# Behind the expert loop: fewer returned rows summed on TensorE, turned tiles copied out by ScalarE

## The reference

```
x = x + gt2 * moe_ffn(modulate(rmsnorm(x, g_ffn[l]), ...), ...)   # 6 of 64 experts a token, and a shared one
...
return rmsnorm(x, g_final)                                        # end of first_block
...
xn = rmsnorm_2(h, norm_mix_g)                                     # start of second_block
proj = jnp.einsum('bsd,de->bse', xn, w_in) + b_in
```

## Time and profile before

| | |
|---|---|
| three runs | 2151.91, 2157.5 and 2158.29 us; median 2157.5 us |
| the profiled execution | 2153.83 us, span 2152.1 us |
| mean granted TensorE clock | 0.992 of full speed |
| busy share of the span | TensorE 95%, VectorE 46%, ScalarE 18%, GpSimd 10% |
| the stretch behind the expert loop | from about 1203 us to the barrier's end at 1259.6 us |

### The profile page before, as it was taken

One profiled execution on the slowest core, in us unless ns is written; L12 is line 12 of the kernel. 1 busy time (PEld: TensorE's weight loads), 2 busy tenths in 40 slices (PEclk: granted clock), 3 DMA queues, 4 the chain that ended last, 5 costly groups with the idle time before them and its releaser, 6 DMA issues. The chain is left out here.

```text
span 2152.1 us, 34202 instructions
## 1 busy us (share of the span) xinstructions
PE 2053.5 (95%) x13624; PEld 1343.3 (62%) x13624; DVE 981.1 (46%) x2048; ACT 384.0 (18%) x832; POOL 213.8 (10%) x281
## 2 busy tenths in 40 slices
PE   6999999999889999999999989999999999999998
PEld 2455567885456666666666444555888668885443
DVE  2554346654532222222222388543655354546564
ACT  3113434441211111111111120111111110000000
POOL 7000023420001111111111000000000000000000
PEclk9999999999999999999999999999999999999999
DMA  9631010020459999999999632103222222223442
GB/s 393 255 118 39 1 41 3 3 74 17 163 223 401 422 421 413 408 403 399 390 387 362 273 151 83 60 30 118 79 79 79 78 79 79 109 87 137 176 172 102
DMA packets 56444, 392.99 MB, mean 183 GB/s; under 512 B 11864, under 2 KB 11992, under 8 KB 21008
## 3 DMA queue, kind: packets, MB, share of 16 engines
q1 hardware_dynamic: 43376, 366.02, 43.1%
q0 software_dynamic: 12960, 25.42, 3.1%
HBM read 385.93 MB, written 27.26 MB: 192 GB/s over the span
## 5 line engine op out<-in xcount | busy, mean ns | idle before, releaser
L2251 PE MATMUL bank<-arena 128*128 128x512 f32 x448 | 198.2, 600 | 2.4 <-SPq L2224 2.4
L2347 PE MATMUL bank<-arena 128*128 128x256 f32 x896 | 194.1, 379 | 0.5 <-DVE arena L2838 0.5
L2418 PE MATMUL bank<-arena 128*128 128x256 f32 x896 | 193.6, 379 | 0.1
L2458 PE MATMUL bank<-arena 128*128 128x512 f32 x448 | 192.7, 592 | 0.1
L2347 PEld LDWEIGHTS bank<-arena 128*128 128x128 f32 x896 | 170.1, 190 | 24.8 <-DVE arena L2838 0.9
L2418 PEld LDWEIGHTS bank<-arena 128*128 128x128 f32 x896 | 170.2, 190 | 23.3 <-issue 0.3
L1662 PE MATMUL bank<-arena 128*64 128x256 f32 x704 | 159.8, 381 | 19.8 <-DMA arena<-in_wexp 14.6
L1649 PE MATMUL bank<-arena 128*128 128x128 f32 x1408 | 163.0, 276 | 2.5 <-ACT arena L1755 0.3
L1649 PEld LDWEIGHTS bank<-arena 128*128 128x128 f32 x1408 | 158.9, 191 | 7.6 <-issue 6.9
L1664 PE MATMUL bank<-arena 128*64 128x256 f32 x704 | 160.3, 382 | 0.0
L2458 PEld LDWEIGHTS bank<-arena 128*128 128x128 f32 x448 | 85.1, 190 | 107.2 <-issue 106.2
(11 more groups left out here) (582 smaller groups left out, 2849.1 us busy)
## 6 DMA issues: line engine op xcount, KB each, us to landing
arena<-in_wexp SPq DMA_DIRECT2D x198, 1024.0 KB, 19.6
arena<-in_w2f SPq DMA_DIRECT2D x24, 2048.0 KB, 7.4
arena<-in_wmod SPq DMA_DIRECT2D x12, 2048.0 KB, 9.0
arena<-in_w2j SPq DMA_DIRECT2D x8, 2048.0 KB, 7.4
arena<-in_win SPq DMA_DIRECT2D x6, 2048.0 KB, 10.9
arena<-expert_rows SPq DMA_DIRECT2D x12, 1024.0 KB, 15.7
arena<-in_w2t SPq DMA_DIRECT2D x8, 1536.0 KB, 6.5
arena<-in_x SPq DMA_DIRECT2D x2, 2048.0 KB, 10.1
```

Source lines behind the costliest of these rows:

```text
L2251: mm = pe.matmul(bk, wv[:, k, :], rhs[:, k, :], start=(k == 0), stop=(k == nk - 1))
L2347: mm = pe.matmul(bk[:, 0:HT], lhs[:, k, :], right[:, k, :], start=(first and k == 0), stop=(k == nk - 1), skip_group_check=not last or not ...
L2418: mm = pe.matmul(b[:, 0:HT], lhs(k), rhs(k), start=(first and k == 0), stop=(k == 3), skip_group_check=not last or not first)
L2458: mm = pe.matmul(b[:, :], lhs(f), rhs(f), start=(g % 8 == 0 and f == 0), stop=(g % 8 == 7 and f == 1))
```

## The change

Two things are moved. First, TensorE sums rows 0, 1 and 2 of a tile, and VectorE adds row 3 itself, ahead of its other adds. Second, the copying out of the turned tiles goes to ScalarE: since its scale is one value per partition, and each block of 128 columns has its own column of `g2`, a tile takes eight instructions of 128 x 128 in place of two of 128 x 512. They stand, for the tile before, ahead of the scaled copy of the row (`xr`). Of the last tile ScalarE copies the second bank, and VectorE the first.

```diff
                 for c in range(2):
                     pe.wait_ge(S(f"yd_in{t}{c}"), 16)
                     for half in range(2):
-                        for k in (2 * c, 2 * c + 1):
-                            mm = pe.matmul(bank[2 * t + half][:, :], ident, y[:, k, 512 * half:512 * half + 512], start=False, stop=(k % 2 == 1),
+                        for k in ((0, 1), (2,))[c]:
+                            mm = pe.matmul(bank[2 * t + half][:, :], ident, y[:, k, 512 * half:512 * half + 512], start=False, stop=(k >= 1),
                                            skip_group_check=True)
...
+            def turned_out(t, ks):
+                for k in ks:
+                    act.wait_ge(S("xn1_mm"), 2 * t + k // 4 + 1)
+                    act.activation(tail_xnT[:, k, t * P:(t + 1) * P], bank[2 * t + k // 4][:, (k % 4) * P:(k % 4 + 1) * P], ACT.Copy, scale=col2("g2", k))
+
...
                 act.wait_ge(S("tail_rs"), t + 1)
+                if t >= 1:
+                    turned_out(t - 1, range(KD))
                 act.activation(xr[:, t, :], xs[:, t, :], ACT.Copy, scale=tail_rs[:, t, 0:1]).then_inc(S("tail_xr"), 1)
+            turned_out(NT_X - 1, range(4, KD))
...
                 y = yslot[t].rearrange("p (k d) -> p k d", k=TOP_K)
+                dve.wait_ge(S(f"yd_in{t}1"), 16)
+                link(dve.tensor_tensor(xr[:, t, :], xr[:, t, :], y[:, 3, :], ALU.add))
                 dve.wait_ge(S(f"yd_in{t}2"), 16)
...
             def turned_out(t):
-                for c in range(2):
+                for c in range(1):
                     dve.wait_ge(S("xn1_mm"), 2 * t + c + 1)
...
             for t in range(NT_X):
                 rows(t)
-                if t >= 1:
-                    turned_out(t - 1)
                 norms(t)
             turned_out(NT_X - 1)
```

## The result

The changed kernel takes 2158.9 us (median of 21 runs, 2153.13 to 2161.69), the kernel before 2155.35 (21 runs beside them, 2150.38 to 2158.3). The ratio is 1.0016 with a 95% interval of 1.0009 to 1.0023, so 3.4 us more, between 1.9 and 5.0: slower, by less than the 0.3% named in the prediction.

A forecast was written before the change was run, and what follows sets the result against it. TensorE, busy for 95% of the span, was taken as the bound, nearly balanced with VectorE behind the expert loop. +1.08 and +0.65 made +1.7 us, on 2155.7 giving 2157.5 us, range 2151.5 to 2163.

The forecast's parts named there:

- The steps: Times between VectorE's first bank adds of successive tiles: forecast 9.6, 8.7, 8.7 us, each with a 1.25 us add.
- T0: Start of VectorE's first bank add of tile 0: forecast 1.72 us earlier, TensorE having four passes less.
- T3: Start of VectorE's first bank add of tile 3: forecast 1.08 us later, 1249.61 instead of 1248.53.
- The small copy: ScalarE's 128x128 copy from PSUM with a scale pointer: taken at 0.32 us each, hidden while under 0.52.
- the end: Last copy out of the last turned tile, by ScalarE: forecast T3 + 10.16 instead of T3 + 9.51, so +0.65 us.
- The clock before the last turn: TensorE's granted clock in the last tile's turn: kept at 0.50 (1.2 GHz), after some 6.8 us idle.
- rival 2: Clock falls to 0.50 before tiles 1 and 2's turns, next phase 1.7 us longer: +5.3 us in all; chance 0.17.
- the clock term behind the barrier: Low clock in the next phase's first 80 TensorE passes: left as before, bounds -1.7 and +1.7 us.
- the sum: Whole change forecast: +1.08 us at T3 and +0.65 at the end, giving +1.7 us.
- the middle of all four: Base time 2155.7 us, from the profiled execution (2153.8) and three shown runs (2151.9, 2157.5, 2158.3).
- Rival 1: Losing the copies relieves VectorE behind the expert loop, run faster: -0.8 us, at best -3.3; chance 0.14.
- rival 3: ScalarE becomes the bound beyond 0.52 us a copy: +8.1 us at 0.68, decides from 0.62; chance 0.03.

The follow-up runs named there:

- The kernel with the sums alone: Against the kernel before: VectorE adds row 3, TensorE sums three rows, all copies stay on VectorE; ratio 1.0011 (1.0002 to 1.0021).
- the one with the copies alone: Against the changed kernel: TensorE sums four rows again, copies stay moved to ScalarE; ratio 1.0008 (0.9999 to 1.0016).
- The first comparison: First profile of the changed kernel against the first of the kernel before: the next phase's first 80 TensorE passes differ by 1.14 us.

## Why the prediction was right and wrong

**The steps.** Right to 0.05 us: T0 1.72 earlier (1.73), one add of 1.25 in the open for three tiles, 0 for the copies, T3 1.08 later (1.12). The kernel with the sums alone shows that the copies were covered by the wait for ScalarE, the one with the copies alone that their removal shows up as a wait of 1.22 us.

**ScalarE.** The small copy was mis-sized twice over. First, 0.317 is not how far apart L866's instructions are. They come in groups of four, and 15.2 / 48 counts the whole last one of each group:

```profile
292.74 1.27 ACT L866 ACTIVATE arena<-arena 128x128 f32<-128x128 f32 x4
```

(1.27 - 0.39) / 3 is 0.29 each. Second, L866 reads SBUF. The copies from PSUM take 2.17 us for eight in a row, the next instruction starting 2.01 behind the first: 0.25 each. The Trainium skill ("ScalarE: Activation LUTs", What ACT_TABLE_LOAD costs) gave 0.29 as an estimate. L866 agrees with that; of the copies from PSUM the single instruction agrees (0.386 by the page, 0.381 in the row below), but the overlap of two is 0.13 here instead of 0.093. The group by shape:

```profile
L1772 ACT ACTIVATE arena<-bank,arena 128x128 f32<-128x128 f32 x28 | 7.7, 381 | 1.7 <-PE bank L1710 1.0 <-DVE arena L2048 0.7
```

For tile 2's eight copies the error costs nothing, since ScalarE waits 0.96 us for the turn anyway. The last four took 1.14 instead of 1.34, and the turn 3.79 instead of 3.68, so the end is 10.06 behind T3 instead of 10.16, with 0.65 forecast and 0.55 measured.

**The clock before the last turn.** 0.50 was kept, and it was 0.50 (3.79 us for the turn). The first half of rival 2 did not come: the gaps of 0.9 us before the turn of tile 0 and of 1.5 before those of tiles 1 and 2 left it at 1.00.

**The step that failed** is the clock term behind the barrier, and with it the size of the sum. The sum took the term at 0 ("leave the 1.7 us of the next phase as it is"), with 1.7 to either side and no reason for the middle. Up to the barrier the sum was right, +1.73 forecast and +1.67 measured. The timed runs differ by 3.4 us (1.9 to 5.0). Everything behind the 80 passes takes the same time, so 0.2 to 3.3 us are left for the 80 passes, unless the stretch ahead of L1703 differs on the average too. The first comparison showed 1.1 us there, the three profiles of each kernel 0.4.

That the cost there comes of TensorE's idle time is shown: with the changed kernel's sums and copies the 80 passes take 34.53 where it was filled before and behind the turn, and 37.61 where only before. That the changed kernel spends more time at 0.50 on the average is shown by the clocks of the timed runs. What makes up the rest of the 3.4 us, beside 1.67 up to the barrier and some 0.4 in the 80 passes, stays open.

**From the sum to the number** a second step failed. The sum of +1.7 us was laid on 2155.7, "the middle of all four", and so gave "2157.5 us", which is the very median shown for the kernel before. As a number this says no change, where the text says slower. The base itself was good (21 runs give 2155.35; the median of the first three was 2.1 too high), and the measured median missed the number by 1.4 us because the change was 3.4 and not 1.7. Laid on the stated median the sum would have given 2159.2, close to the measured 2158.9, but by luck: the base too high by about as much as the change was too small. Base and change are better given apart, each with its own range.

**Rival 1** (relief, faster) is refuted, **rival 3** (ScalarE the bound) too, with 0.25 against the 0.62 where it decides. Of **rival 2** the part before 1250 did not come; of the 1.7 us in the next phase the profiles show 0.4.

## What to carry over

Before moving work off an engine, look at what its next instruction waits for when that work is gone. Here two copies filled a wait of their own length, so taking them away bought a wait, and the add put in exchange stood in the open, three times. Moving work between two nearly balanced engines pays tile by tile: two rows to VectorE at the first tile alone, where it waits for TensorE, moved the last sum 3.1 us forward; one row at every tile moved it 1.1 us back. A term of which the rows give only bounds, here the clock behind an idle stretch, needs a reason for its middle, too: it was taken at nothing, and the time moved by twice the sum.

## What the runs showed of the hardware

In eleven of the fourteen profiles TensorE had an idle stretch of 3.4 to 6.7 us before or behind the last turn, and in all eleven the granted clock was 0.50 (1.2 GHz) in the turn or in the next phase's first passes. Where the slow stretch begins and ends differs between executions of one kernel: the 80 passes took 36.22 to 37.37 us in the changed kernel and 36.23 to 37.27 in the one before. In the three profiles in which matmuls without a use left no idle stretch there longer than 2.4 us, the clock stayed at 1.00, the turn took 2.05 instead of 3.1 to 3.8, and the 80 passes 34.53 or 34.54. And with a scale pointer, ScalarE copies of 128x128 in a row started 0.25 us apart from PSUM and 0.29 from SBUF (L866), though one alone takes 0.38 to 0.39 in either case.
